# GpSimd takes the low part of every second weight slot of a gate projection, and the steps of a triangular inverse are dealt out by their elements

## What is computed

```
h = x + 0.5 * rms_norm(swiglu_ffn(rms_norm(x)))
proj = rms_norm(h) @ w_in          # rw_seg | q, k, v | gate_a, gate_b
y_a = rwkv7_branch(token_shift(rw_seg))   # recurrence in both directions
y_b = diff_attention_branch(q, k, v)
merged = sigmoid(gate_a) * (y_a @ w_branch_a) + sigmoid(gate_b) * (y_b @ w_branch_b)
h = h + rms_norm(merged @ w_out)
h = h + 0.5 * rms_norm(swiglu_ffn(rms_norm(h)))
```

## Time and profile before

| what | us |
|---|---|
| device time, three runs | 2579.11, 2579.84, 2584.63 |
| median | 2579.84 |
| span of the profiled execution | 2576.5 |
| TensorE matmul busy | 2403.1 (93%) |
| VectorE busy | 1413.1 (55%) |
| ScalarE busy | 1060.9 (41%) |
| GpSimd busy | 127.6 (5%) |
| last GpSimd item before the gate stage's own work: load of z issued | at 1157.58 |
| last step of the inverse ends | near 1329.65 |
| VectorE's first instruction of the recurrence | at 1373.16 |

### The profile page before, as it was taken

One profiled execution on the slowest core, in us unless ns is written; L12 is line 12 of the kernel. 1 busy time (PEld: TensorE's weight loads), 2 busy tenths in 40 slices (PEclk: granted clock), 3 DMA queues, 4 the chain that ended last, 5 costly groups with the idle time before them and its releaser, 6 DMA issues.

```text
span 2576.5 us, 31948 instructions
## 1 busy us (share of the span) xinstructions
PE 2403.1 (93%) x12010; PEld 1951.7 (76%) x12010; DVE 1413.1 (55%) x1672; ACT 1060.9 (41%) x1393; POOL 127.6 (5%) x177
## 2 busy tenths in 40 slices
PE   7999999999989999889797976789899999999997
PEld 5888888888868885667576854678688888888885
DVE  4454444544554474988973445465554444445454
ACT  5444434444444464444232224344544443444442
POOL 0000000000000001320001130000000000000000
PEclk9999999999999998899898987899999999999998
DMA  6666666666557664556473023366566666666664
GB/s 225 193 188 189 188 195 191 193 187 188 187 188 214 184 190 133 148 167 213 138 214 105 10 84 84 98 215 192 158 195 187 188 187 194 195 191 187 189 186 131
DMA packets 225605, 443.78 MB, mean 172 GB/s; under 512 B 22574, under 2 KB 24796, under 8 KB 223836
## 3 DMA queue, kind: packets, MB, share of 16 engines
q1 hardware_dynamic: 206720, 397.72, 52.2%
q0 software_dynamic: 9488, 39.76, 4.6%
q10 hardware_dynamic: 9292, 4.87, 0.7%
HBM read 423.42 MB, written 18.87 MB: 172 GB/s over the span
## 4 chain that ended last, share of the span: by engine, by line
PE 83%; DVE 12%; ACT 2%; DMA 2%; issue 1%; POOL 0%; SPq 0%; DVEq 0%; ACTq 0%; POOLq 0%
PE ps L1263 25%; PE ps L1264 24%; PE ps L1265 24%; DVE wlo L776 3%; DVE z L1019 2%; DVE zt L1014 2%; DMA raw<-in_w_in 1%; PE ps L1301 1%; PE ps L1471 1%; PE ps L1430 1%; PE ps L1456 1%; PE ps L1284 1%; PE ps L1446 1%; PE ps L1472 1%; DVE h L833 1%
## 5 line engine op out<-in xcount | busy, mean ns | idle before, releaser
L776 DVE TENSOR_TENSOR wlo<-raw,whi 128x1024 fp32r<-128x1024 f32 (+1 forms) x760 | 929.8, 1226 | 974.0 <-ACT whi L442 971.7
L442 ACT ACTIVATE whi<-raw 128x1024 fp32r<-128x1024 f32 (+1 forms) x760 | 802.9, 1059 | 1146.2 <-PE ps L1265 1056.3
L1263 PE MATMUL ps<-whi,uhi 128*128 128x512 f32 (+1 forms) x2208 | 875.5, 397 | 29.4 <-DVE wlo L776 29.4
L1264 PE MATMUL ps<-wlo,uhi 128*128 128x512 f32 (+1 forms) x2208 | 866.9, 393 | 0.0
L1265 PE MATMUL ps<-whi,ulo 128*128 128x512 f32 (+1 forms) x2208 | 866.3, 392 | 0.0
L1263 PEld LDWEIGHTS ps<-whi,uhi 128*128 128x128 f32 x2208 | 419.8, 190 | 131.4 <-DVE wlo L776 37.0
L1265 PEld LDWEIGHTS ps<-whi,ulo 128*128 128x128 f32 x2208 | 419.7, 190 | 87.7
L1264 PEld LDWEIGHTS ps<-wlo,uhi 128*128 128x128 f32 x2208 | 420.0, 190 | 84.0
L1263 PE MATMUL ps<-whi,hthi 128*128 128x512 f32 x704 | 274.2, 389 | 0.0
L1265 PE MATMUL ps<-whi,htlo 128*128 128x512 f32 x704 | 273.9, 389 | 0.0
L1264 PE MATMUL ps<-wlo,hthi 128*128 128x512 f32 x704 | 273.9, 389 | 0.0
(11 more groups left out here) (260 smaller groups left out, 1492.9 us busy)
## 6 DMA issues: line engine op xcount, KB each, us to landing
raw<-in_ffn_w_gu SPq DMA_DIRECT2D x352, 512.0 KB, 3.7
raw<-in_ffn_w_down SPq DMA_DIRECT2D x176, 512.0 KB, 3.9
raw<-in_w_in SPq DMA_DIRECT2D x160, 512.0 KB, 3.7
raw<-in_w_out SPq DMA_DIRECT2D x32, 512.0 KB, 4.6
raw<-in_w_branch_a SPq DMA_DIRECT2D x16, 512.0 KB, 4.9
raw<-in_w_branch_b SPq DMA_DIRECT2D x16, 512.0 KB, 4.1
gate_dram<-gst_g POOLq DMA_DIRECT2D x8, 512.0 KB, 4.9
gbuf<-gate_dram POOLq DMA_DIRECT2D x8, 512.0 KB, 4.2
```

What stands on the lines that cost most here:

```text
L442: nc.scalar.activation(whi[:, s, :, 0:p.width], raw[:, s, :, 0:p.width], ACT.Copy).then_inc(hi_ready, 1)
L776: V.tensor_tensor(wlo[:, s, :, 0:p.width], raw[:, s, :, 0:p.width], whi[:, s, :, 0:p.width].bitcast(F32), ALU.subtract).then_inc(lo_ready, 1)
L1263: mm(o, at, w_, start=(j == 0 and k == 0), stop=False)
L1264: mm(o, at, l_, start=False, stop=False)
```

## The change

Three edits belong together. First, GpSimd makes the low parts of slots 5, 7, ..., 59 of the gate projection (28 slots), counted by a semaphore of its own, `lo_pool`; VectorE skips them. Who waits for a low part (SyncE, TensorE) now picks the right semaphore and count with `wait_lo`, and for that the loops of SyncE and TensorE over the gate slots are written out instead of looped. Second, the steps of the inverse are dealt out between slots 8 and 55 by 160 + s(63-s) instead of by number. Third, GpSimd's order changes: after each of its low parts of slots 13, 21, ..., 53 stands the store of a gate chunk, and the wait for `z_done` and z's store now stand behind its low part of slot 59.

```diff
+        GATE_SLOTS = p_gate.chunks * p_gate.slots
+        POOL_SLOTS = range(RING + 1, GATE_SLOTS - RING, 2)
+
+        def wait_lo(eng, p, n):
+
+            k = n - p_gate.n0 if isinstance(n, int) else None
+            if k is not None and 0 <= k < GATE_SLOTS:
+                before = len([s for s in POOL_SLOTS if s <= k])
+                if k in POOL_SLOTS:
+                    eng.wait_ge(lo_pool, before)
+                else:
+                    eng.wait_ge(lo_ready, n + 1 - before)
+            else:
+                eng.wait_ge(lo_ready, n + 1 - (len(POOL_SLOTS) if p.n0 > p_gate.n0 else 0))
...
-                        sp.wait_ge(lo_ready, n - RING + 1)
+                        wait_lo(sp, p, n - RING)
...
-                walk(sp, p, load)
+                if p is p_gate:
+                    for _ in in_steps(p, load, [], []):
+                        pass
+                else:
+                    walk(sp, p, load)
...
+            STEP_WORK = [160 + s * (C - 1 - s) for s in range(C - 1)]
...
-                return min(max(k - first, 0) * (C - 1) // (last - first), C - 1)
+                share = min(max(k - first, 0) / (last - first), 1)
+                return next(i for i in range(C) if sum(STEP_WORK[:i]) >= share * sum(STEP_WORK) - 1)
...
-                if k >= RING:
+                if k >= RING and k not in POOL_SLOTS:
...
-                    pe.wait_ge(lo_ready, n + 1)
+                    wait_lo(pe, p, n)
...
-            walk(pe, p_gate, from_u(p_gate, None))
+            for _ in in_steps(p_gate, from_u(p_gate, None), [], []):
+                pass
...
-            store_gates(range(6))
+            def pool_lo(k):
+                s = (p_gate.n0 + k) % RING
+                pool.wait_ge(hi_ready, p_gate.n0 + k + 1)
+                G.tensor_tensor(wlo[:, s, :, :], raw[:, s, :, :], whi[:, s, :, :].bitcast(F32), ALU.subtract).then_inc(lo_pool, 1)
+
+            for k in POOL_SLOTS:
+                pool_lo(k)
+                if k > p_gate.slots and k % p_gate.slots == 5:
+                    store_gates([k // p_gate.slots - 1])
             pool.wait_ge(z_done, 1)
```

More of the change, by code:

```diff
@@ L283, in layer @@
         lo_ready = sem("lo_ready")
+        lo_pool = sem("lo_pool")
         slots_used = sem("slots_used")
```

## The result

The changed kernel takes 2600.21 us (median of 4 runs, 2598.84 to 2600.96) against 2581.49 for the kernel before (4 runs): a ratio of 1.0072, 95% interval 1.0058 to 1.0086. It is 18.7 us slower. The profiled execution took 2599.57 us with a span of 2597.8, 21.3 above the span of before; up to 1145 the two traces are alike.

What follows compares the result with a forecast made beforehand. VectorE was taken to bound the kernel from z's arrival to the last step, TensorE before that. The terms 20.7 - 2.5 - 6.1 gave +12.1 us on 2579.84, so 2591.9, range 2583 to 2605.

Steps and rivals of the forecast that it cites:

- Rival B: VectorE's stretch: a GpSimd low part costs only 1.37 to 1.83 us, time within 0.2%, some 2580; chance 8%.
- Rival C: Gate stage: TensorE, idling more, drops to its lower clock and becomes the bound; +13 us, 2605; chance 10%.
- rival A: Gate stage: GpSimd and VectorE work side by side, so the kernel gets faster, 2543 us; chance 9%.
- The loss per low part: z's arrival to last step: 23 low parts of 1.23 removed, 23 blocks of 2.13 added; net +20.7 us.
- The even deal: Steps of the inverse: moving them between slots changes no sum of VectorE's work; 0 us.
- The late start: Slot 5: TensorE loses 1.7 to 2.9 us, covered because VectorE waits for z until 1166.4; 0 us.
- Stores and written-out loops: Later chunk stores, loops written out for SyncE and TensorE, one more semaphore: 0, with 1 us either way.
- The end of the stage: Last step to recurrence: slot 55 sooner after z_done, -2.5 us; slot 63's stall gone, recurrence sooner after slot 55, -6.1.

Runs made afterwards that it cites:

- e3: Kernel before, VectorE keeping all low parts, plus 28 unused two-input GpSimd operations of 128x1024 ahead of z's store: 2628.39 us against 2580.50, ratio 1.0173.
- e4: Changed kernel with the product tile of the inverse in PSUM instead of SBUF: 2582.07 us against 2580.50 for the kernel before, ratio 1.0004.
- e8: Kernel before, VectorE keeping all low parts, plus 28 unused one-input GpSimd copies of 128x1024: 2595.35 us against 2581.04, ratio 1.0060.
- e1: Kernel before with only the steps of the inverse dealt out by elements, VectorE making all low parts: 2579.53 us against 2580.50, ratio 0.9993.
- e6: Changed kernel with GpSimd making only the low parts of slots 5 to 53: 2600.82 us against 2581.04 for the kernel before, ratio 1.0086.
- e9: Kernel before with only z's store held until VectorE has made the low part of slot 59: 2577.16 us against 2580.02, ratio 0.9990.

## Why the prediction was right, and what was mis-sized

The forecast was 2591.9, slower, in a range of 2583 to 2605; measured are 2600.2. Of the 8.3 us between them, 6.6 are the change, which cost 18.7 instead of 12.1, and 1.7 are the kernel before, at 2581.49 in this comparison instead of 2579.84. The forecast's own ends were 2587 to 2599, and 2600.2 lies just outside them; it is in the range because that was drawn wide enough for rivals B and C, and neither of them came in. The mechanism is the one forecast, and e3, e4 and e8 leave no room for rival A (side by side) or for a cause in the handing over. Point by point:

1. **The loss per low part, +20.7.** Measured +26.8 in the stretch (190.1 against 163.3). The price of an operation was right: 2.12, with 2.13 forecast. Two other factors were mis-sized. There were 25 operations in the stretch, not 23: GpSimd does not wait for VectorE's order and made slots 55 and 57 before VectorE's last step, which brings a loss of 4.2 us and saves VectorE nothing there. I had counted the slots by VectorE's program, where slot 54 is the last ahead of the final step, and not by when GpSimd would get to them. And a low part taken away was worth 1.14, not its length of 1.23: 26.2 us for 23 instead of 28.3. The row of two low parts in 2.36 us already showed it, since 1.14 + 1.23 is 2.37. Together: 25 x 2.12 - 23 x 1.14 = 26.8, and of the 6.1 us missing 4.2 are the count and 2.1 the length, less 0.2 for the price of 23 operations.
2. **The even deal, 0.** Right: e1, 0.9993 (0.9983 to 1.0003).
3. **The late start, 0.** Right: TensorE was busy 19.8 of 21.0 us up to 1166.4, so it lost about 1.2, and the steps began at 1166.02, with z.
4. **Stores and written-out loops, 0.** No sign of a cost: the loss per operation is the same 2.12 in the changed kernel and in e3, which has the stores moved but the loops as they were. This was not tried by itself.
5. **The end of the stage, -8.6.** Measured -6.4. No stall at slot 63, as said, and the store came 5.3 after the last step where 7.0 was reckoned. But the transfers took longer: 10.3 to the issue of zs instead of 9.3, and the recurrence started 21.5 after that issue instead of 18.7 (31.5 less 3.5 and 9.3). That the order decides whether slot 63's load is late is shown by e6 from one side and by e9 from the other.

Terms 1 and 5 give 26.8 - 0.3 - 6.4 = 20.1 at the recurrence (0.3 because z came that much earlier); the medians show 18.7, and where the 1.4 between them lies is open.

The Trainium skill (SBUF — State Buffer, SBUF: two separate sides) calls the pair of ports that VectorE and GpSimd share an exclusive lock, and names two SBUF inputs on VectorE's side as one condition. The runs agree: 2.0 to 2.2 us whatever the size of the held instruction, and no add held once one of its inputs lies in PSUM (e4). Taken to the letter, the whole instruction, the page gave 2.34 per operation; the trace has 2.12.

Rival C (TensorE bound by its clock) did not come in. The granted clock fell to 0.90 from 0.94, but VectorE was busy 185.6 of 189.8 us between z's arrival and the last step, with no more idle time than before. Rival B needed at most 1.83 per operation, and the changed kernel has 2.12; only e4, with its products in PSUM, comes under it.

## What to carry to other kernels

An idle GpSimd is not free help for a busy VectorE: where both would run operations with two SBUF inputs, moving one of 128x1024 elements takes 1.14 us of work away and brings a loss of 2.12. Where VectorE had no breaks, as here, that did not pay. Giving part of VectorE's work an input from PSUM lowers the loss (1.51 in e4) but did not turn it into a gain here. Whether it pays where VectorE has breaks was not tried. Look for this in the trace before the change: any VectorE operation that is two or three times its usual length beside a GpSimd one gives the price. Count the operations by when the other engine will get to them, and value what is taken away by the distance between two starts, not by its length. And where a long transfer stands at the end of a stage, look at which weight load it travels beside: sending it early is not always best (e6).

## What I had not expected

- Sending z's store 10 us earlier (e6, 1351.70 against 1361.39) moved the recurrence 2.4 us later, since slot 63's load then travelled beside the loads of zs and ScalarE waited 12.4 us for it. The last step had even come 4.7 earlier.
- A GpSimd copy with a single SBUF input holds VectorE up too, 0.77 us of its 1.04.
- How constant the price is. The extra length of a held operation does not depend on its size: the add of 62 elements took 2.51 us instead of 0.28, the multiply of 128x950 took 3.35, against 1.15 for its add.
